# Seven half-size products for each gate and up pair of the second block's feed-forward blocks

## What is computed

```python
for l in range(DEPTH):
    mod = jnp.split(c_act @ w_ada[l] + b_ada[l], N_MOD, axis=-1)
    h = modulate(rms_norm_2(x, ffn1_norm[l]), mod[0], mod[1])
    x = x + FFN_RESIDUAL * (1 + mod[2])[:, None, :] * swiglu_2(h, ffn1_w_gu[l], ffn1_w_down[l])
    ...  # the mixer
    h = modulate(rms_norm_2(x, ffn2_norm[l]), mod[6], mod[7])
    x = x + FFN_RESIDUAL * (1 + mod[8])[:, None, :] * swiglu_2(h, ffn2_w_gu[l], ffn2_w_down[l])

def swiglu_2(h, w_gu, w_down):
    g, u = jnp.split(h @ w_gu, 2, axis=-1)
    return (jax.nn.silu(g) * u) @ w_down
```

## Time and profile before

| | us |
|---|---|
| median of 3 runs | 3531.23 |
| lowest and highest | 3527.92, 3532.91 |
| span of the profiled execution | 3529.6 |
| PE busy | 3498.3 |
| DVE busy | 2067.0 |
| ACT busy | 1307.9 |
| POOL busy | 63.8 |

### The profile page before, as it was taken

One profiled execution on the slowest core, in us unless ns is written; L12 is line 12 of the kernel. 1 busy time (PEld: TensorE's weight loads), 2 busy tenths in 40 slices (PEclk: granted clock), 3 DMA queues, 4 the chain that ended last, 5 costly groups with the idle time before them and its releaser, 6 DMA issues.

```text
span 3529.6 us, 45935 instructions
## 1 busy us (share of the span) xinstructions
PE 3498.3 (99%) x17160; PEld 2837.1 (80%) x17160; DVE 2067.0 (59%) x3447; ACT 1307.9 (37%) x2145; POOL 63.8 (2%) x122
## 2 busy tenths in 40 slices
PE   9999999999999999999999999999999999999999
PEld 7777777888876788888888887888888887878887
DVE  5777776666876566685334767433443347673334
ACT  5555554222343332333323444323332234442222
POOL 0000000000000000000000000000000000000000
PEclk9999999999999999999999999999999999999999
DMA  4222223656421365652232212323323322223232
GB/s 145 85 65 78 76 65 106 216 200 206 168 71 49 108 200 194 206 187 94 96 95 93 80 66 73 103 99 96 95 90 97 99 91 77 72 73 100 94 101 79
DMA packets 142102, 387.35 MB, mean 110 GB/s; under 512 B 21680, under 2 KB 63024, under 8 KB 141936
## 3 DMA queue, kind: packets, MB, share of 16 engines
q1 hardware_dynamic: 127024, 306.65, 27.1%
q0 software_dynamic: 14912, 78.52, 6.5%
HBM read 382.11 MB, written 2.10 MB: 109 GB/s over the span
## 4 chain that ended last, share of the span: by engine, by line
PE 95%; DVE 3%; issue 1%; ACT 1%; DMA 0%; SPq 0%; DVEq 0%; ACTq 0%
PE psP L1127 26%; PE psP L1132 25%; PE psP L1128 25%; PE psP L1278 3%; PE psP L1285 3%; PE psP L1279 3%; PE psS L1624 1%; PE psM L1647 1%; PE psS L1341 1%; PE psS L1507 1%; PE psS L1310 1%; PE psS L1323 0%; PE psS L1491 0%; PE psS L1329 0%; PE psS L1635 0%
## 5 line engine op out<-in xcount | busy, mean ns | idle before, releaser
L1127 PE MATMUL psP<-h_hi,w_hi 128*128 128x512 f32 x2664 | 1052.5, 395 | 4.8 <-ACT h_hi L734 2.3
L1128 PE MATMUL psP<-h_hi,w_lo 128*128 128x512 f32 x2664 | 1037.7, 390 | 0.0
L1132 PE MATMUL psP<-h_lo,w_hi 128*128 128x512 f32 x2664 | 1027.8, 390 | 0.0
L1740 DVE TENSOR_TENSOR w_lo<-raw,w_hi 128x1024 fp32r<-128x1024 f32 (+1 forms) x456 | 546.7, 1199 | 396.5 <-ACT w_hi L678 390.4
L684 ACT ACTIVATE ybuf<-psP 128x512 f32<-128x512 f32 (+1 forms) x401 | 239.4, 597 | 1199.5 <-PE psP L1132 1198.1
L1127 PEld LDWEIGHTS psP<-h_hi,w_hi 128*128 128x128 f32 x2664 | 500.5, 188 | 127.2 <-issue 25.8
L1132 PEld LDWEIGHTS psP<-h_lo,w_hi 128*128 128x128 f32 x2664 | 498.3, 188 | 107.7 <-DVE h_lo L1818 4.2
L1128 PEld LDWEIGHTS psP<-h_hi,w_lo 128*128 128x128 f32 x2664 | 500.8, 188 | 99.4
L678 ACT ACTIVATE w_hi<-raw 128x1024 fp32r<-128x1024 f32 (+1 forms) x456 | 471.0, 1033 | 65.4 <-PE psP L1132 65.4
L1127 PE MATMUL psP<-a_hi,w_hi 128*128 128x512 f32 x1248 | 486.3, 390 | 1.2 <-ACT a_hi L1080 1.2
L1128 PE MATMUL psP<-a_hi,w_lo 128*128 128x512 f32 x1248 | 485.6, 389 | 0.0
(11 more groups left out here) (336 smaller groups left out, 3545.9 us busy)
## 6 DMA issues: line engine op xcount, KB each, us to landing
raw<-in_gu SPq DMA_DIRECT2D x264, 512.0 KB, 3.3
adaw<-in_ada POOLq DMA_DIRECT2D x96, 768.0 KB, 5.7
raw<-in_down SPq DMA_DIRECT2D x96, 448.0 KB, 3.3
raw<-in_down SPq DMA_DIRECT2D x48, 512.0 KB, 3.6
raw<-in_qkv SPq DMA_DIRECT2D x40, 512.0 KB, 3.6
raw<-in_mix_in SPq DMA_DIRECT2D x34, 512.0 KB, 3.2
raw<-in_qkv SPq DMA_DIRECT2D x64, 256.0 KB, 3.1
raw<-in_wo SPq DMA_DIRECT2D x32, 512.0 KB, 3.3
```

The source lines that it names most:

```text
L1127: nc.tensor.matmul(psP[:, s, :], hi, rhs[0](kt), start=(n == 0), stop=False)
L1128: nc.tensor.matmul(psP[:, s, :], lo, rhs[0](kt), start=False, stop=False)
L1132: mm = nc.tensor.matmul(psP[:, s, :], w_hi[:, s, kt * P:kt * P + P], rhs[1](kt), start=False, stop=(n == K - 1))
L1740: v.tensor_tensor(w_lo[:, s, 0:cols], raw[:, s, 0:cols], w_hi[:, s, 0:cols].bitcast(F32), ALU.subtract)\
```

## The change

The first 3 of the 22 pairs of a block stay as they were. For the other 19 (`PAIRS`) the product of one pair is seen as a matrix of 2 by 2 blocks: outputs gate and up, inner dimension in two halves of 4 `kt`, tokens in two halves of 256. Seven products of block sums take the place of eight products of blocks. `PRODUCTS` lists them as PSUM bank, weight operand, input operand; each has 4 `kt` and 3 matmuls, 128x256: 84 matmuls for a pair in place of 48 of 128x512.

The sums have to be made. Of the inputs: `norm` now keeps its scaled tiles in `t_early` and `t_late`, and DVE forms four sums of each of 4 tiles (`token_sums`), which ACT and DVE split into `ht_hi` and `ht_lo`, once in a block. Of the weights, for each pair: SP loads pieces of 256 KB into `s_raw`; POOL issues two transfers that add a second piece from memory onto S1 and S3 (`weight_sums`); DVE adds twice more (`sum_2`, `sum_4`). The six operands and A22, which takes the place of A11, are split in four groups: highs on ACT, lows on DVE. Of the outputs: ACT copies bank states into `st_c` after products 1, 5, 6 and 7, DVE adds three times (`gate_late`, `up_late`, `gate_early`), ACT applies Silu, DVE multiplies twice (`activated`), ACT and DVE split the result.

The parts are smaller (`SEVEN_PARTS`), and the 8 down tiles of a part are spread over the pairs of the next one, in frames. PE's order in a frame is products 1, 5, 6, 3, one down tile, products 7, 2, 4, and the remaining one or two down tiles. DVE takes a down tile straight from PSUM into `xT` (`added`), so ACT no longer evacuates it. The 8 down tiles of the last part follow at the end.

```diff
+SEVEN_PARTS = ((0, 3), (3, 4), (7, 4), (11, 4), (15, 3), (18, 4))
+PLAIN = SEVEN_PARTS[0][1]
+PAIRS = FT - PLAIN
+HK, HT = 4, T // 2
+A11, S1, S2, S4, S3, A12 = range(6)
+A22 = A11
+PRODUCTS = (("A", A11, "b11"), ("E", S1, "t1"), ("A", S2, "t2"), ("E", S4, "b22"), ("A", S3, "t3"), ("B", A12, "b21"), ("A", A22, "t4"))
+P1, P5, P6, P3, P7, P2, P4 = range(1, 8)
+G2, G1, G3, G4 = range(1, 5)
...
+def seven_frames():
+    frames = []
+    for n, (f0, nf) in enumerate(SEVEN_PARTS[1:]):
+        for j in range(nf):
+            first, end = -(-KT * j // nf), -(-KT * (j + 1) // nf)
+            frames.append((n + 1, f0 + j, [(n, m) for m in range(first, end)]))
+    return frames
...
+                def load_s1(q):
+                    if q < PAIRS:
+                        if F.pair(l, q):
+                            sp.wait_ge(*s_low.at(low(q - 1, G1)))
+                        sp.dma_start(s_raw[:, S1, :], up_of(q)[:, 0:T]).then_inc(s_landed["s1"].sem, 16)
...
+                def load_a11(q):
+                    if q < PAIRS:
+                        if F.pair(l, q):
+                            sp.wait_ge(*s_low.at(low(q - 1, G4)))
+                        sp.dma_start(s_raw[:, A11, :], gate_of(q)[:, 0:T]).then_inc(s_landed["a11"].sem, 16)
+                def load_s3_a12(q):
+                    if q < PAIRS:
+                        if F.pair(l, q):
+                            sp.wait_ge(*s_low.at(low(q - 1, G3)))
+                        sp.dma_start(s_raw[:, S3, :], up_of(q)[:, 0:T]).then_inc(s_landed["s3"].sem, 16)
+                        sp.dma_start(s_raw[:, A12, :], gate_of(q)[:, T:2 * T]).then_inc(s_landed["a12"].sem, 16)
+                def load_a22(q):
+                    if q < PAIRS:
+                        sp.wait_ge(*s_low.at(low(q, G1)))
+                        sp.dma_start(s_raw[:, A22, :], up_of(q)[:, T:2 * T]).then_inc(s_landed["a22"].sem, 16)
...
+                for q, (_, _, tiles) in enumerate(frames):
+                    load_a11(q + 1)
+                    down_load()
+                    load_a22(q + 1)
+                    load_s1(q + 2)
+                    load_s3_a12(q + 2)
+                    for _ in tiles[1:]:
+                        down_load()
+...
+            def weight_sums(F, l):
+                for q in range(PAIRS):
+                    tile = l * 2 * FT + 2 * (PLAIN + q)
+                    pool.wait_ge(*s_landed["s1"].at(16 * (F.pair(l, q) + 1)))
+                    pool.dma_start(s_raw[:, S1, :], F.gu[tile + 1][:, T:2 * T], accum_op=ALU.add).then_inc(s1_added.sem, 16)
+                    pool.wait_ge(*s_landed["s3"].at(16 * (F.pair(l, q) + 1)))
+                    pool.dma_start(s_raw[:, S3, :], F.gu[tile][:, 0:T], accum_op=ALU.add).then_inc(s3_added.sem, 16)
...
+                def highs_2(q):
+                    act.wait_ge(*s_summed.at(2 * F.pair(l, q) + 2))
+                    if q:
+                        product_done(q - 1, P3)
+                    highs_of(S2, 2)
+                def highs_1(q):
+                    act.wait_ge(*s_landed["a11"].at(16 * (F.pair(l, q) + 1)))
+                    act.wait_ge(*s1_added.at(16 * (F.pair(l, q) + 1)))
+                    if q:
+                        product_done(q - 1, P4)
+                    highs_of(A11, 2)
...
+                    copied(q, P1, "A", C1)
+                    highs_4(q)
+                    copied(q, P5, "E", C5)
+                    copied(q, P6, "A", C2)
+                    pos.step()
+                    ahead()
+                    copied(q, P7, "A", C3)
+                    if more:
+                        highs_2(q + 1)
+                    act.wait_ge(*s_joined.at(3 * F.pair(l, q) + 3))
+                    nc.scalar.activation(st_c[:, q % 2, C1:C1 + 2, :], st_c[:, q % 2, C1:C1 + 2, :], ACT.Silu).then_inc(s_silu.sem, 1)
+                    if more:
+                        highs_1(q + 1)
+                    act.wait_ge(*s_gated.at(2 * F.pair(l, q) + 2))
+                    slot = a_place(n) + f - SEVEN_PARTS[n][0]
+                    nc.scalar.activation(a_hi[:, slot, :], st_c[:, q % 2, C1:C1 + 2, :].rearrange("p a t -> p (a t)"), copy)\
+                        .then_inc(s_a_high.sem, 1)
+                    if more:
+                        highs_3(q + 1)
+                    for _ in tiles[1:]:
+                        pos.step()
+                        ahead()
+                nc.scalar.activation(warm[:, :], ident[:, 0:1], ACT.Sqrt)
...
+                def product(p):
+                    name, slot, src = PRODUCTS[p - 1]
+                    fresh = p in (P1, P5, P2)
+                    for k in range(HK):
+                        hi, lo = s_hi[:, slot, k * P:k * P + P], s_lo[:, slot, k * P:k * P + P]
+                        high, low = moving[src](h_hi, ht_hi, k), moving[src](h_lo, ht_lo, k)
+                        start, stop = fresh and k == 0, k == HK - 1
+                        nc.tensor.matmul(bank[name], hi, high, start=start, stop=False, skip_group_check=True)
+                        nc.tensor.matmul(bank[name], lo, high, start=False, stop=False, skip_group_check=True)
+                        mm = nc.tensor.matmul(bank[name], hi, low, start=False, stop=stop, skip_group_check=True)
+                    mm.then_inc(s_product.sem, 1)
...
+                for q, (n, f, tiles) in enumerate(seven_frames()):
+                    pair = F.pair(l, q)
+                    pe.wait_ge(*s_low.at(4 * pair + G1))
+                    if q:
+                        pe.wait_ge(*s_gated.at(2 * pair))
+                    product(P1)
+                    if q == 0:
+                        pe.wait_ge(t_low, 2 * HK * (F.turn(l) + 1))
+                    product(P5)
+                    pe.wait_ge(*s_copied.at(4 * pair + 1))
+                    product(P6)
+                    pe.wait_ge(*s_copied.at(4 * pair + 2))
+                    product(P3)
+                    for d, m in tiles[:1]:
+                        if d > a_waited:
+                            pe.wait_ge(F.a_ready, l * FT + sum(SEVEN_PARTS[d]) + 1)
+                            a_waited = d
+                        down(d)
+                    pe.wait_ge(*s_low.at(4 * pair + G3))
+                    pe.wait_ge(*s_copied.at(4 * pair + 3))
+                    product(P7)
+                    product(P2)
+                    pe.wait_ge(*s_low.at(4 * pair + G4))
+                    pe.wait_ge(*s_copied.at(4 * pair + 4))
+                    product(P4)
+                    for d, m in tiles[1:]:
+                        down(d)
...
+                    nt1, t3, t2, nt4 = (st_c[:, k % 2, i, :] for i in range(4))
+                    v.tensor_tensor(nt1, z[:, early], z[:, late], ALU.subtract).then_inc(t_summed, 1)
+                    v.scalar_tensor_tensor(t3, zl[:, late], shift_step[:, k:k + 1], z[:, late], ALU.add, ALU.subtract).then_inc(t_summed, 1)
+                    dve.wait_ge(t_summed, before + 2)
+                    v.scalar_tensor_tensor(t2, z[:, early], sh(k), t3, ALU.add, ALU.add).then_inc(t_summed, 1)
+                    dve.wait_ge(t_summed, before + 3)
+                    v.scalar_tensor_tensor(nt4, zl[:, early], sh(HK + k), t2, ALU.add, ALU.subtract).then_inc(t_summed, 1)
...
+                def added(m):
+                    dve.wait_ge(tile_done, pos.count(RING + 1))
+                    v.scalar_tensor_tensor(xT[:, m, :], psP[:, pos.slot(), :], gate_col(m), xT[:, m, :], ALU.mult, ALU.add)\
+                        .then_inc(evac_done, 1)
+                    pos.step()
...
+                token_sums(0)
+                token_sums(1)
+                token_lows(0)
+                token_lows(1)
+                plain_pair(0)
+                token_sums(2)
...
+                for q, (n, f, tiles) in enumerate(frames):
+                    more = q + 1 < PAIRS
+                    lows(q, G4, A22, 1)
+                    gate_late(q)
+                    added(tiles[0][1])
+                    ahead()
+                    if more:
+                        sum_2(q + 1)
+                    up_late(q)
+                    if more:
+                        sum_4(q + 1)
+                    gate_early(q)
+                    if more:
+                        lows(q + 1, G2, S2, 2)
+                    activated(q)
+                    if more:
+                        lows(q + 1, G1, A11, 2)
+                    a_low(q, n, f)
+                    if more:
+                        lows(q + 1, G3, S3, 2)
+                    for _, m in tiles[1:]:
+                        added(m)
+                        ahead()
+                    if q == 1 and between:
+                        between()
...
+                for m in range(KT - 1):
+                    added(m)
+                    dve.wait_ge(evac_done, pos.count(RING))
+                    squares(N, m, xT[:, m, :], acc)
+                    ahead()
```

(23 more changed lines are left out.)

232 lines of the change are left out of this document (212 added, 20 removed).

## The result

| | before | after |
|---|---|---|
| median | 3529.57 | 3571.02 |
| lowest and highest of 4 runs | 3527.88, 3532.91 | 3570.77, 3571.26 |
| span of the profiled execution | 3529.6 | 3568.9 |

The account below looks back on a forecast made before the run. PE's matmul row alone bounds the blocks. Frames -8.0, head +4.4, tail +1.65 give -1.95 us a block, -7.8 for four: 3521.8 in the span, 3523.4 as median, stated as 3524, range 3485 to 3605.

Parts of the forecast that it names:

- The bound and the place: PE's matmuls bound the blocks before; after, PE waits before the next pair's product 1 for DVE's lows of group 1.
- the walk: DVE's instructions added up in one frame, from the inner down tile to the lows of group 1, 7.61 us.
- I take 0.1133: PE's 256-column matmuls: half of 0.2267 us each, range 0.111 to 0.120, saving 1.36 us a pair.
- Its own alternative: PE's matmuls: the 0.0133 us above 512 columns is fixed for each matmul, so 256 columns take 0.120 us.
- +24 us: The 48 matmuls in front of the inner down tile, in 76 frames, if each takes 0.0067 us more.
- I cost it at nothing, if the added transfer is in time: DMA transfers for the weight pieces: some 2.7 MB in 15.5 us a frame, taken to make nothing wait.
- rival 1: POOL's added transfer into S1 lands late for `sum_2`, deciding from about 5.5 us; about 3595 at 7 us; chance 17%.
- 175 GB/s: Mean DMA rate forecast for a frame, some 2.7 MB in 15.5 us, against 211 GB/s moved without PE waiting.
- The head: Start of a block: token sums delay tile 3 by 2.8 us and product 1 of pair 0 by 1.3; 4.4 a block.
- The second wait of 1.3: Before product 1 of pair 0: `sum_2` to group 1 stand behind two more token sums, about 1.3 us.
- The tail: Last 8 down tiles of a block: DVE falls behind PE by 1.65 us when the norm begins.
- Rival 2: DVE's row in the frame doesn't bind, PE does, so all 103 us but head and tail are gained: about 3450; 8%.

Follow-up runs that it names:

- The first experiment: The kernel before the change, its 128x512 matmuls cut into 256+256, 384+128 and 4 x 128 columns in three feed-forward blocks, each piece with its own weight load: 3992.99 us.
- The last kernel: Against the kernel with S1 split earlier and A22 in its own buffer (3500.77 us): head work in PE's order, first pair's A22 loaded early: 3485.03 us, ratio 0.9881.

## Why the prediction was wrong

**The bound and the place: right; the size of the row partly by luck.** PE's row set the time before, and what took its place is the row on DVE that was named, from the inner down tile to the lows of group 1. The frame above has 7.55 us for 7.61, but 0.2 of it is a wait for the transfer that the walk had at nothing. With the adding left out the row takes 7.33 and 7.36 in the mean, so the walk was 0.25 to 0.3 too long (the two instructions of `activated` take 0.66 for its 0.78, for one), 17 us over the 64 frames that it was meant for. In the changed kernel it takes 7.90 in frames with 3 `kt` and 7.50 in those with 4. The two errors nearly cancel, and 4 us more than forecast are left.

**"I take 0.1133" failed, the step on the matmuls.** Its own alternative held: the part above the columns is fixed for a matmul, 0.120. I leaned on the rows of 64 and 128 columns with as many weight loads, which start 0.111 to 0.112 apart. The first experiment shows that 128 columns lie on a floor of 0.1116, which tells nothing about 256 columns; the row of 512 columns did, read as columns and a fixed part. The price was in the text, +24 us, of the 47 that are missing. In the trace it is a little more: four products in front of the inner down tile take 5.75 us, and 5.86 when PE has waited before them, for 5.44, so 0.42 x 17 + 0.31 x 2 = 7.8 us a block, 31 in all.

**"I cost it at nothing, if the added transfer is in time" failed in part, which is rival 1.** The transfer takes 6.0 us in the median, over the 5.5 from which the rival decides. S1's landed at 3.84 - 0.34 = 3.5 rather than 3.3. It is late in 27 of the 72 frames, and leaving the adding out gives 21 us back, 16 of them in the 28 frames with 3 `kt`, where `sum_2` wants it 0.7 us earlier. The rival's size, 68 us, was taken for 7 us of transfer and every frame. The forecast and the rival weren't alternatives: both rows, DVE's and the transfers', end within a few tenths of a microsecond of each other in most frames. The mean rate was no guide to this: the forecast had 175 GB/s (with 0.9 MB of down tiles a pair, which are 0.4 to 0.8), the trace has 128 to 133 over a block, and one transfer is late all the same.

**The head: the sum nearly right, its parts not.** PE waited 3.8 us for tile 3 in the first block and 2.4 to 2.5 in the others (2.8 forecast). The second wait of 1.3 did not come but for 0.5 in the last block. In its place three of the blocks had PE at the lower of its two clocks behind the wait, below. Together 15.8 us for 17.6. That the sum is near is luck.

**The tail: 1.65 us forecast, 2.1 to 2.8 in three blocks and 0.2 in the last, 7.5 for 6.6.** In the first block the last 105 matmuls and the wait behind them take 24.9 us for 23.8, and the norm behind is 7.2 long for 6.2.

**The sum, remade** from all 76 frames of the trace, against the forecast. The 48 matmuls in front of the inner down tile and what PE lost among them: 40 us, 31 for the price of a matmul, 3.4 for waits on the ACT copies, about 4 for the lower clock, the rest small. DVE's row: 4. The down tiles, and the frames in which PE doesn't wait: 5 to 6. Head and tail: -2 and +1. That is 49 us for a miss of 47. Either of the two failed terms, 31 for the matmuls or 21 for the adding, turns the forecast gain of 7 into a loss.

**Rival 2** (nothing but PE binds) was 3531 - 103 + 24 = 3450; with 0.1199 the same sum is 3531 - 62 + 24 = 3493. The last kernel, in which orders and buffers are changed and the sums and products are not, runs at 3485, below that; its heads, with the first frame, cost about 1.3 us each for the 4.4 in this sum. The order hid what the change is worth.

## What to carry to other kernels

The price of a smaller instruction has a fixed part and a floor; take the row of the same kind with other sizes, and split it, before you halve it. When a buffer is loaded only after its last reader and two transfers follow each other into it, draw the circle from one read to the next: here an earlier read only waited longer, and splitting one operand earlier (S1 apart) was worth more than moving the sums. Where an instruction needs two transfers, look in the trace which of them landed last before you name the circle. An order on one engine is also the release order of what others wait for; each wait taken away uncovers the next, so expect two or three rounds.

## What the runs showed of the hardware

A wait of PE can cost more than its length. Behind the wait for tile 3 the timeline of the changed kernel shows starts 0.427 us apart (four steps from 1618.90 to 1620.61) instead of 0.227:

```profile
1617.88 0.80 PE L1375 MATMUL psP<-h_hi,w_hi 128*128 128x512 f32 x1 [3.76 <-DVE w_lo L2048]
...
1618.90 0.63 PE L1380 MATMUL psP<-h_lo,w_hi 128*128 128x512 f32 x1
...
1620.61 0.45 PE L1375 MATMUL psP<-h_hi,w_hi 128*128 128x512 f32 x1
```

The granted clock of that stretch is 0.50, which is 1.2 GHz, and 1.00 again in the second one:

```profile
1617.80:1620.00 2.20, 2.12 (x5) 1.73 (x6) 2.17 (x4) 0.20 (x1) 0.00 (x0) 0.50 0.77 157
...
1623.00:1626.00 3.00, 3.00 (x15) 2.48 (x14) 2.93 (x6) 2.49 (x5) 0.00 (x0) 1.00 0.00 0
```

From 1617.88 to 1620.61 it is 2.73 us for 6 steps that take 1.36 at 2.4 GHz: 1.4 us on top of 3.8. Two of the three waits of 2.4 to 2.5 us were followed by the same, the last one not. It came inside the frames too: behind a wait of 3.34 us before product 1 at 2536.38, and behind one of 2.19 us at 2668.22, but not behind one of 2.77 us at 2287.86.

```profile
2537.00:2542.00 5.00, 5.00 (x25) 5.00 (x25) 3.01 (x4) 1.32 (x4) 0.00 (x0) 0.50 0.34 105
2669.00:2671.50 2.50, 2.50 (x13) 2.50 (x13) 2.16 (x3) 0.71 (x3) 0.00 (x0) 0.50 0.77 231
```

The four products behind the first of these took 8.44 us and those behind the second 7.34, for 5.86. So the length of the wait alone does not tell whether the clock falls.
